# Half of each expert's down product in the full format, and three smaller moves

## The chip, the cores and the metric

One Trainium2 chip; the program runs on one of its cores. The metric is the device time of one execution, in microseconds (us). Before the change three runs gave 3543.78, 3550.85 and 3563.93 us, median 3550.85. Engines: PE (TensorE; PEld is its weight load), DVE (VectorE), ACT (ScalarE), POOL (GpSimd), SP (SyncE, which here issues the weight transfers).

## The reference, cut to what matters

One sequence of 256 tokens of width 1024 goes through a first block (a mixer, then a mixture of experts) and four layers of a second model, each of a gated feed-forward, a mixer and another gated feed-forward. Three parts matter here:

```
hdn = silu(einsum('td,edf->tef', xc, w1)) * einsum('td,edf->tef', xc, w3)   # experts, f = 256
y   = einsum('tef,efd->td', hdn * gate, w2)                                 # 128 tokens at a time
def rms_norm(x, g):     return x * rsqrt(mean(x * x, -1) + eps) * g
def swiglu(h, wi, wo):  a, b = split(h @ wi); return (silu(a) * b) @ wo     # 2816 hidden, 8 times
```

All weights are float32. Each token picks one of 4 groups of 8 experts and two experts in it.

## The kernel before, in words

**Split products.** A float32 matrix product is made of three matmuls in a reduced format, fp32r. The weights w are split into a high part (ACT copies w into a tile of type fp32r, which rounds) and a low part (DVE subtracts the high part from w); the activations are split in the same way. PE then adds high times high, high times low and low times high (`three`, L1857 in the experts, L1008 in the feed-forward). A matmul on plain float32 tiles, which needs no split, appears in the trace as two records of the same line.

**The expert stage** (`moe_stage`). 40 units: five windows of 128 token places, eight experts each. A unit's weights are 128 x 6144 floats (3 MB): four up pieces of 1024 columns (b = 0 to 3) and two down pieces (b = 4, 5), one for each half of the 256 hidden numbers. SP loads unit j + 2 into a ring of 4 slots when ACT has said that unit j - 2's slot is free (`act.nop()` at L2075, waited for in `load_ahead`, L443). Per unit j, in the written order of each engine:
- PE: up piece 0 (6 matmuls of 128 x 512), the transpose of the previous unit's hidden numbers (`turn_hidden`, L1872), up pieces 1 to 3, then `down_products(j - 1)`: two pieces, 6 matmuls each. After some units come `gather` (L1912), `turn_places` and `scatter_half` (L1926), in plain float32, for the next or the last window of tokens.
- ACT: high part of up piece 0, silu (L2000), high parts 1 to 3 (`high_part`, L1996), the nop that frees a slot, `hidden_high(j - 1)` (L2006), the high parts of the two down pieces of j - 1, then the issue of two transfers of 512 KB on its own queue (`load_quarters`, L2048).
- DVE: low part of up piece 0 (`low_part`, L2115), `product` (L2128), low parts 1 to 3, `hidden_low` (L2133), low part of down piece 4, one quarter sum, low part of down piece 5, one quarter sum. A quarter sum (L582) is a 128 x 1024 product of the adaptive-norm weights of layer 0 that has nothing to do with the experts; units 2 to 37 do two each, from the 512 KB transfers.
- The high parts sit in 4 tiles, used in turn by piece number: `up_piece` and `down_piece` give the number, 6 per unit, and ACT waits until piece number - 4 has been multiplied (`piece_used`).
- POOL adds each scattered half window to x (L2100).

**Root norm between stages** (`NextNorm` of kind "root", 12 places). ACT squares the eight chunks of x (L797), POOL adds them in pairs (`pair_sums`, L699, 128 x 256), PE sums each pair over features with a column of ones (`token_sums`, L711, 2 matmuls a pair), then DVE (L755), ACT, DVE (L758) and PE (`spread_tokens`, L720) make the inverse root and spread it; the next stage starts after that.

**The feed-forward stage** (`glu_stage`, 8 times, 11 units each). At its start PE clears four banks with matmuls on zeros (L1060, 4 of 128 x 512), then runs `first_up_products` (L1025): another zero matmul (L1027), pieces 0 and 1 chunk by chunk as DVE finishes each chunk of the normed input (`u_low`, L1231), then pieces 2 and 3. `up_products(1, 1)` and `down_products(0, 1)` follow; the latter is the first to add into the four cleared banks. Three of the eight stages (those before the mixers of layers 0 to 2) issue four transfers on ACT's queue during unit 1.

## Time and profile before

| | |
|---|---|
| median of three runs | 3550.85 us |
| the profiled execution | 3549.21 us, span 3547.4 us |
| PE busy | 3181.7 us, 90% |
| DVE busy | 2334.2 us, 66% |
| ACT busy | 1579.0 us, 45% |
| POOL busy | 145.4 us, 4% |
| mean granted TensorE clock | 0.924 of full |
| expert stage, units | about 280 to 726 us of the span |
| read from HBM | 690.27 MB, 196 GB/s over the span |

Time of PE is a union of overlapping matmuls: a record lasts from its start until its result is out, and the next one starts earlier. The pace of a row of matmuls is read from the difference of two starts, not from a duration. The same holds for ACT and DVE to a lesser degree.

### The profile page before, as it was taken

How to read it: one execution, taken by the hardware profiler on the slowest of the kernel's cores; microseconds unless marked ns; L12 is line 12 of the kernel's file. 1: busy time of each engine (PE TensorE's matmuls, PEld its weight loads, DVE VectorE, ACT ScalarE, POOL GpSimd, SP SyncE). 2: the span in 40 equal slices, each digit the busy share in tenths (PEclk: the TensorE clock that was granted, in tenths of full speed). 3: DMA queues.
4: the chain of work that ended last, by engine and by line, in shares of the span. 5: the costliest groups of instructions: out<-in, count | busy, mean ns of one | idle time of the engine just before them, and what ended most of it. 6: DMA issues, size and time to landing. Idle time of an engine off the chain costs nothing. (4 is left out here: it accounts for less than half of the span.)

```text
span 3547.4 us, 62682 instructions
## 1 busy us (share of the span) xinstructions
PE 3181.7 (90%) x26368; PEld 2947.7 (83%) x26368; DVE 2334.2 (66%) x3480; ACT 1579.0 (45%) x2254; POOL 145.4 (4%) x160
## 2 busy tenths in 40 slices
PE   7679888889897889999987799999899998978899
PEld 6577666679886789999985799999699998867899
DVE  6548899957765457677575467676667645655544
ACT  3426666644452244444552344444544444432443
POOL 0000000000101100000000000000000001011000
PEclk9869999989997989999995899999899999979899
DMA  9347999947620047677440167575157444200242
GB/s 388 128 160 277 355 381 381 366 190 304 241 97 37 2 157 305 238 279 306 156 163 1 72 230 308 227 303 214 39 201 307 187 178 174 109 37 3 107 178 83
DMA packets 74358, 697.79 MB, mean 197 GB/s; under 512 B 8080, under 2 KB 12176, under 8 KB 50704
## 3 DMA queue, kind: packets, MB, share of 16 engines
q1 hardware_dynamic: 31216, 532.99, 38.1%
q10 hardware_dynamic: 41760, 153.11, 11.5%
q0 software_dynamic: 1152, 8.39, 0.6%
q8 instruction: 173, 2.83, 0.3%
q14 instruction: 57, 0.47, 0.0%
HBM read 690.27 MB, written 4.19 MB: 196 GB/s over the span
## 5 line engine op out<-in xcount | busy, mean ns | idle before, releaser
L1171 DVE TENSOR_TENSOR w_split<-ring,w_split 128x1024 fp32r<-128x1024 f32 x513 | 625.7, 1223 | 446.5 <-ACT w_split L1082 444.1
L1082 ACT ACTIVATE w_split<-ring 128x1024 fp32r<-128x1024 f32 x513 | 540.2, 1056 | 769.8 <-PE banks L1012 605.8
L1010 PE MATMUL banks<-u_split,w_split 128*128 128x256 f32 x2816 | 802.5, 285 | 10.8 <-DVE u_split L1231 5.7
L1011 PE MATMUL banks<-u_split,w_split 128*128 128x256 f32 x2816 | 800.2, 284 | 0.0
L1012 PE MATMUL banks<-u_split,w_split 128*128 128x256 f32 x2816 | 800.0, 284 | 0.0
L1010 PEld LDWEIGHTS banks<-u_split,w_split 128*128 128x128 f32 x2816 | 544.8, 193 | 15.1 <-DVE w_split L1171 11.1
L1011 PEld LDWEIGHTS banks<-u_split,w_split 128*128 128x128 f32 x2816 | 544.4, 193 | 0.6
L1012 PEld LDWEIGHTS banks<-u_split,w_split 128*128 128x128 f32 x2816 | 544.0, 193 | 0.0
L582 DVE CUSTOM_DVE_ANT_0 bufs<-bufs 128x1024 f32<-128x1024 f32 x332 | 396.0, 1224 | 46.5 <-DMA bufs<-ada 32.6
L1010 PE MATMUL banks<-h_split,w_split 128*128 128x256 f32 x1408 | 398.7, 283 | 1.3 <-DVE w_split L1171 1.3
L1011 PE MATMUL banks<-h_split,w_split 128*128 128x256 f32 x1408 | 398.4, 283 | 0.0
L1012 PE MATMUL banks<-h_split,w_split 128*128 128x256 f32 x1408 | 398.4, 283 | 0.0
L518 PE MATMUL banks<-bufs_split,ring_split 128*128 128x256 f32 x1312 | 380.1, 290 | 0.0
L516 PE MATMUL banks<-bufs_split 128*128 128x256 f32 x984 | 292.8, 298 | 54.1 <-DVE ring_split L504 36.1
L2115 DVE TENSOR_TENSOR ring_split<-ring,bufs_split 128x1024 fp32r<-128x1024 f32 x240 | 296.0, 1260 | 19.1 <-ACT bufs_split L1996 18.9
L517 PE MATMUL banks<-bufs_split 128*128 128x256 f32 x936 | 274.6, 293 | 0.0
L1996 ACT ACTIVATE bufs_split<-ring 128x1024 fp32r<-128x1024 f32 x240 | 250.0, 1062 | 52.3 <-PE banks L1862 48.1
L1010 PEld LDWEIGHTS banks<-h_split,w_split 128*128 128x128 f32 x1408 | 270.3, 192 | 1.9 <-issue 1.9
L1012 PEld LDWEIGHTS banks<-h_split,w_split 128*128 128x128 f32 x1408 | 270.3, 192 | 0.0
L1011 PEld LDWEIGHTS banks<-h_split,w_split 128*128 128x128 f32 x1408 | 270.3, 192 | 0.0
L518 PEld LDWEIGHTS banks<-bufs_split,ring_split 128*128 128x128 f32 x1312 | 261.9, 200 | 0.0
L516 PEld LDWEIGHTS banks<-bufs_split 128*128 128x128 f32 x984 | 199.1, 202 | 64.4 <-DVE ring_split L504 39.3
(466 smaller groups left out, 5120.2 us busy)
## 6 DMA issues: line engine op xcount, KB each, us to landing
ring<-stream SPq DMA_DIRECT2D x155, 3072.0 KB, 11.0
bufs<-ada ACTq DMA_DIRECT2D x288, 512.0 KB, 10.4
bufs<-ada SPq DMA_DIRECT2D x7, 2048.0 KB, 11.7
bufs<-ada POOLq DMA_DIRECT2D x8, 1024.0 KB, 7.9
ring<-stream SPq DMA_DIRECT2D x2, 2688.0 KB, 9.8
bufs<-c_rows SPq DMA_DIRECT2D x8, 512.0 KB, 4.5
ring<-stream SPq DMA_DIRECT2D x1, 2704.0 KB, 12.5
ring<-stream SPq DMA_DIRECT2D x1, 2176.0 KB, 9.0
```

The lines of the kernel that those rows point to most:

```text
L516: pe.matmul(out, w_high, x_high, start=start, stop=False, skip_group_check=True)
L517: pe.matmul(out, w_high, x_low, start=False, stop=False, skip_group_check=True)
L518: return pe.matmul(out, w_low, x_high, start=False, stop=stop, skip_group_check=True)
L582: dve.tensor_tensor_reduce(w, w, c_row, 1.0, 0.0, ALU.mult, ALU.add, into).then_inc(done.sem, 1)
L1010: pe.matmul(out, w(0), x(0), start=start, stop=False, skip_group_check=True)
L1011: pe.matmul(out, w(0), x(1), start=False, stop=False, skip_group_check=True)
L1012: return pe.matmul(out, w(1), x(0), start=False, stop=stop, skip_group_check=True)
L1082: nc.scalar.activation(w_split[:, slot, 0, :], piece(j, b), ACT.Copy).then_inc(high.sem, 1)
L1171: e = nc.vector.tensor_tensor(w_split[:, slot, 1, :], piece(j, b), w_split[:, slot, 0, :].bitcast(F32), ALU.subtract)
L1996: act.activation(w_high[number % 4], piece(j, b), ACT.Copy).then_inc(high.sem, high.count(1))
L2115: dve.tensor_tensor(low_piece(j, b), piece(j, b), w_high[number % 4].bitcast(F32), ALU.subtract)\
```

## The change

Four edits. In the expert stage the second down piece (b = 5) is no longer split: PE multiplies it as plain float32, with the lower half of the turned hidden numbers copied by ACT to a plain float32 tile (`turned_f32`). Pieces are now numbered 5 per unit, `down_done` counts units whose down product is complete, and the nop that frees a ring slot stands behind `hidden_high(j - 1)`. In the root norm, POOL adds three pairs, and PE sums chunks 6 and 7 directly (`paired_sums`). In the feed-forward stage the four bank-clearing matmuls stand behind `first_up_products`.

```
-    for q in range(KC // 2):
+    for q in range(pairs):                      # NextNorm "root" passes pairs=KC // 2 - 1
...
+def paired_sums(core, pe, squares, bank, paired, squared, summed):
+    ones = core.const("ones")[:, 0:1]
+    for c in (0, 2, 4, 6, 7):
+        if c < KC - 2:
+            pe.wait_ge(paired.sem, paired.at(c // 2 + 1))
+        else:
+            pe.wait_ge(squared.sem, squared.at(c + 1))
+        for t in range(2):
+            last = pe.matmul(core.psum[:, bank + t, 0:1], squares[:, c, t * P:(t + 1) * P], ones, start=(c == 0), stop=(c == KC - 1))
+    last.then_inc(summed.sem, summed.count(1))
...
+            first_up_products()
             for b in range(4):
                 pe.matmul(core.psum[:, 4 + b, :], core.zeros[:, 0:P], core.zeros[:], start=True, stop=True)
-            first_up_products()
...
+    turned_f32 = [core.bufs[:, 8, (4 + 2 * q) * SEQ + P:(5 + 2 * q) * SEQ] for q in range(2)]
...
     def up_piece(j, b):
-        return 6 * j - 2 + b if j else b
+        return 5 * j - 1 + b if j else b
-    def down_piece(j, f):
-        return 6 * j + 8 + f if j < units - 1 else 6 * units - 2 + f
+    def down_piece(j):
+        return 5 * j + 8 if j < units - 1 else 5 * units - 1
...
+                number = down_piece(j)
+                pe.wait_ge(low.sem, low.at(number + 1))
+                for half in range(2):
+                    last = three(y[:, half, :], weight(number, j, 4, slice(half * 512, (half + 1) * 512)),
+                                 [h_split[:, j % 2, part, 0:P] for part in range(2)], e == 0, False)
+                last.then_inc(piece_used.sem, piece_used.count(1))
+                for half in range(2):
+                    last = pe.matmul(y[:, half, :], turned_f32[j % 2], piece(j, 5)[:, half * 512:(half + 1) * 512],
+                                     start=False, stop=e == E - 1, skip_group_check=True)
+                last.then_inc(down_done.sem, down_done.count(1))
...
-                    act.wait_ge(piece_used.sem, piece_used.at(down_ends(j - 2)))
-                act.activation(h_split[:, j % 2, 0, :], turned(j), ACT.Copy).then_inc(h_high.sem, h_high.count(1))
+                    act.wait_ge(down_done.sem, down_done.at(j - 1))
+                act.activation(turned_f32[j % 2], turned(j)[:, P:2 * P], ACT.Copy)
+                act.activation(h_split[:, j % 2, 0, 0:P], turned(j)[:, 0:P], ACT.Copy).then_inc(h_high.sem, h_high.count(1))
...
-                    if j >= 2:
-                        act.nop().then_inc(core.freed.sem, core.freed.count(1))
                 hidden_high(j - 1)
+                if 2 <= j < units:
+                    act.nop().then_inc(core.freed.sem, core.freed.count(1))
...
-                for f in range(2):
-                    high_part(j - 1, 4 + f, down_piece(j - 1, f))
+                high_part(j - 1, 4, down_piece(j - 1))
...
-                    if i == 1:
-                        low_part(j - 1, 5, down_piece(j - 1, 1))
```

DVE's `hidden_low` handles 128 instead of 256 columns.

ACT's order in one plain unit of the expert stage, before: the last line of the first unit's high parts, then the next unit (L1996 is a high part, L2000 the silu, L2006 `hidden_high`, L2048 the transfers).

```order
L1996 ACTIVATE bufs_split<-ring 128x1024
L2000 ACTIVATE bufs<-banks 128x256
L1996 ACTIVATE bufs_split<-ring 128x1024 x3
L2006 ACTIVATE bufs_split<-banks 128x256
L1996 ACTIVATE bufs_split<-ring 128x1024 x2
L2048 DMA bufs<-ada 128x1024 x2
```

ACT's order there after (L2009 is the high part, L2013 the silu, L2019 the plain copy of the lower half, L2020 the high part of the upper half, L2062 the transfers).

```order
L2009 ACTIVATE bufs_split<-ring 128x1024
L2013 ACTIVATE bufs<-banks 128x256
L2009 ACTIVATE bufs_split<-ring 128x1024 x3
L2019 ACTIVATE bufs<-banks 128x128
L2020 ACTIVATE bufs_split<-banks 128x128
L2009 ACTIVATE bufs_split<-ring 128x1024
L2062 DMA bufs<-ada 128x1024 x2
```

One high part of a weight piece is gone, and one small copy has come. The nop is not a row of this list: before, it stood behind the three high parts; after, it stands behind L2020.

PE's order after where a down product of the expert stage ends and the next unit begins (L1871 to L1873 are the split products, L1914 the plain ones).

```order
L1871 MATMUL banks<-bufs_split 128x512
L1872 MATMUL banks<-bufs_split 128x512
L1873 MATMUL banks<-ring_split_52,bufs_split 128x512
L1914 MATMUL banks<-ring,bufs 128x512 x2
L1871 MATMUL banks<-bufs_split 128x512
```

Before, six rows of L1860 to L1862 stood where L1914's two matmuls stand.

PE's order at the border between a mixer's last stage and a feed-forward stage, before (L711 and L720 are the norm's, L1060 and L1027 the zeros, L1010 to L1012 the products).

```order
L711 MATMUL banks<-consts_sb,bufs 128x1 x8
L720 MATMUL banks<-consts_sb,by_token 128x128 x2
L1702 UNCONDITIONAL_BRANCH
L1006 UNCONDITIONAL_BRANCH
L1060 MATMUL banks<-zeros_split 128x512 x4
L1027 MATMUL banks<-zeros_split 128x512
L1010 MATMUL banks<-u_split,w_split 128x256
```

And after (L725 for L711, L733 for L720, L1040 for L1027, L1023 to L1025 for the products).

```order
L725 MATMUL banks<-consts_sb,bufs 128x1 x10
L733 MATMUL banks<-consts_sb,by_token 128x128 x2
L1715 UNCONDITIONAL_BRANCH
L1019 UNCONDITIONAL_BRANCH
L1040 MATMUL banks<-zeros_split 128x512
L1023 MATMUL banks<-u_split,w_split 128x256
```

The norm has two matmuls more; the four zero matmuls have gone from here and stand 96 products later.

## Rows read from the trace of the kernel before

**Rows 1.** The page: mean busy share of the DMA engines in 40 slices, in tenths.

```profile
DMA  9347999947620047677440167575157444200242
```

**Rows 2.** Eight units: busy of PE, PEld, DVE, ACT, POOL; PEclk, DMA share, GB/s.

```profile
434.67:522.63 87.96, 78.45 (x354) 61.26 (x354) 82.99 (x100) 58.88 (x77) 4.80 (x2) 1.00 0.96 382
```

**Rows 3.** The DMA view of 434.67 to 522.63 us.

```profile
DMA packets 3462, 33.57 MB, mean 382 GB/s; under 512 B 383, under 2 KB 383, under 8 KB 2435
```

**Rows 4.** Timeline of DVE in the expert stage: start us, us, engine, line, operation.

```profile
434.67 0.47 DVE L2128 SCALAR_TENSOR_TENSOR bufs<-bufs,small,banks 128x256 f32<-128x256 f32 x1
435.06 3.49 DVE L2115 TENSOR_TENSOR ring_split<-ring,bufs_split 128x1024 fp32r<-128x1024 f32 x3
...
438.80 1.22 DVE L2115 TENSOR_TENSOR ring_split<-ring,bufs_split 128x1024 fp32r<-128x1024 f32 x1
439.93 1.22 DVE L582 CUSTOM_DVE_ANT_0 bufs<-bufs 128x1024 f32<-128x1024 f32 x1
...
444.50 0.47 DVE L2128 SCALAR_TENSOR_TENSOR bufs<-bufs,small,banks 128x256 f32<-128x256 f32 x1
```

**Rows 5.** Timeline of PE in the expert stage.

```profile
505.16 0.39 PE L1860 MATMUL banks<-bufs_split 128*128 128x512 f32 x1
505.38 0.39 PE L1861 MATMUL banks<-bufs_split 128*128 128x512 f32 x1
...
398.45 1.89 PE L1926 MATMUL banks<-bufs 128*128 128x256 f32 x8
```

**Rows 6.** Waits from 280 to 730 us: total, times, longest.

```profile
PE banks L1860 <- DVE ring_split L2115: 50.1, 55, 5.6
DVE bufs L582 <- DMA bufs<-ada: 7.8, 3, 4.8
```

**Rows 7.** Timeline of ACT, and landing of the ring's transfers (260 to 740 us).

```profile
411.41 1.06 ACT L1996 ACTIVATE bufs_split<-ring 128x1024 fp32r<-128x1024 f32 x1 [1.17 <-PE banks L1862]
413.97 0.39 ACT L2006 ACTIVATE bufs_split<-banks 128x256 fp32r<-128x256 f32 x1 [1.49 <-PE banks L1872]
416.76 1.06 ACT L1996 ACTIVATE bufs_split<-ring 128x1024 fp32r<-128x1024 f32 x1 [0.36 <-PE banks L1862]
...
421.23 1.06 ACT L1996 ACTIVATE bufs_split<-ring 128x1024 fp32r<-128x1024 f32 x1 [0.75 <-PE banks L1862]
...
DMA to landing us min/median/max: 9.9/11.8/13.6
```

**Rows 8.** Timeline of one root norm behind a feed-forward stage.

```profile
946.33 3.16 ACT L797 ACTIVATE bufs<-x_sb 128x256 f32<-128x256 f32 x8 [2.94 <-DVE x_sb L3700]
949.57 0.61 PE L711 MATMUL banks<-consts_sb,bufs 128*128 128x1 f32 x4 [0.18 <-POOL bufs L699]
951.23 0.61 PE L711 MATMUL banks<-consts_sb,bufs 128*128 128x1 f32 x4 [1.06 <-POOL bufs L699]
```

**Rows 9.** The same behind a mixer, and (745 us) behind the centering stage.

```profile
1287.84 0.81 ACT L797 ACTIVATE bufs<-x_sb 128x256 f32<-128x256 f32 x2 [0.93 <-DVE x_sb L2376]
1289.50 0.61 PE L711 MATMUL banks<-consts_sb,bufs 128*128 128x1 f32 x4 [0.60 <-POOL bufs L699]
...
745.00 2.02 PE L711 MATMUL banks<-consts_sb,bufs 128*128 128x1 f32 x8 [0.40 <-POOL bufs L699]
```

**Rows 10.** Feed-forward starts: zeros, first chunk, first product; a wait in unit 1.

```profile
1292.34 2.04 PE L1060 MATMUL banks<-zeros_split 128*128 128x512 f32 x4 [0.32 <-PEq L1702]
1293.46 0.48 DVE L1231 SCALAR_TENSOR_TENSOR u_split<-bufs,mod,u_split 128x256 fp32r<-128x256 f32 x1 [0.25 <-ACT u_split L824]
1294.61 0.41 PE L1010 MATMUL banks<-u_split,w_split 128*128 128x256 f32 x1
...
1513.36 0.39 PE L1010 MATMUL banks<-u_split,w_split 128*128 128x256 f32 x1 [2.24 <-DVE w_split L1171]
```

**Rows 11.** Two stretches of the first such start, columns as in rows 2.

```profile
1294.60:1297.20 2.60, 2.60 (x14) 2.59 (x13) 2.60 (x8) 1.76 (x4) 0.00 (x0) 0.50 1.11 403
1297.20:1300.00 2.80, 2.80 (x25) 2.80 (x25) 1.96 (x5) 1.07 (x3) 0.00 (x0) 0.99 1.00 418
```

More of the change, by code:

```diff
@@ L692, with pair_sums @@
 MEAN_BANK, ROOT_BANK = 2, 3
-def pair_sums(core, pool, squares, squared, paired, per=1, offset=0):
-    for q in range(KC // 2):
+def pair_sums(core, pool, squares, squared, paired, per=1, offset=0, pairs=KC // 2):
+    for q in range(pairs):
         pool.wait_ge(squared.sem, squared.at((2 * q + 2) // per + offset))
@@ L779, in on_gpsimd @@
         if self.kind == "root":
-            pair_sums(self.core, pool, self.squares, self.squared, self.paired)
+            pair_sums(self.core, pool, self.squares, self.squared, self.paired, pairs=KC // 2 - 1)
     def on_tensor(self, pe):
@@ L790, in on_tensor @@
             inverse = core.event("inverse")
-            token_sums(core, pe, self.squares[:, 0:KC:2, :], self.bank, self.paired, self.summed, n=KC // 2)
+            paired_sums(core, pe, self.squares, self.bank, self.paired, self.squared, self.summed)
             pe.wait_ge(inverse.sem, inverse.at(self.turn + 1))
@@ L1809, in up_piece @@
     def up_piece(j, b):
-        return 6 * j - 2 + b if j else b
-    def down_piece(j, f):
-        return 6 * j + 8 + f if j < units - 1 else 6 * units - 2 + f
+        return 5 * j - 1 + b if j else b
+    def down_piece(j):
+        return 5 * j + 8 if j < units - 1 else 5 * units - 1
     def up_ends(j):
         return up_piece(j, 3) + 1
-    def down_ends(j):
-        return down_piece(j, 1) + 1
     def piece(j, b):
@@ L1838, in moe_stage @@
             "u_high", "u_low", "w_high", "w_low", "piece_used", "glu_silu", "glu_hidden", "norm_applied", "h_high", "h_low"))
-        y_done = core.event("glu_down_done")
+        y_done, down_done = core.event("glu_down_done"), core.event("expert_down_done")
         step, ada_loaded = core.event("ada_step"), [core.event(f"ada_loaded{q}") for q in range(4)]
@@ L1895, in down_products @@
                     pe.wait_ge(y_copied.sem, y_copied.at(2 * w))
-                for f in range(2):
-                    number = down_piece(j, f)
-                    pe.wait_ge(low.sem, low.at(number + 1))
-                    for half in range(2):
-                        last = three(y[:, half, :], weight(number, j, 4 + f, slice(half * 512, (half + 1) * 512)),
-                                     [h_split[:, j % 2, part, f * P:(f + 1) * P] for part in range(2)],
-                                     e == 0 and f == 0, e == E - 1 and f == 1)
-                    last.then_inc(piece_used.sem, piece_used.count(1))
+                number = down_piece(j)
[8 more added lines that the diff above has]
+                last.then_inc(down_done.sem, down_done.count(1))
             def gather(w):
@@ L2022, in copy_y @@
             def copy_y(w):
-                act.wait_ge(piece_used.sem, piece_used.at(down_ends(E * w + E - 1)))
+                act.wait_ge(down_done.sem, down_done.at(E * w + E))
                 if w:
@@ L2084, in _ @@
                     scale_y(v - 1, e - 2)
-                for f in range(2):
-                    high_part(j - 1, 4 + f, down_piece(j - 1, f))
+                high_part(j - 1, 4, down_piece(j - 1))
                 if e == 5 and v < WINDOWS - 1:
@@ L2132, in hidden_low @@
                 dve.wait_ge(h_high.sem, h_high.at(j + 1))
-                dve.tensor_tensor(h_split[:, j % 2, 1, :], turned(j), h_split[:, j % 2, 0, :].bitcast(F32), ALU.subtract)\
+                dve.tensor_tensor(h_split[:, j % 2, 1, 0:P], turned(j)[:, 0:P], h_split[:, j % 2, 0, 0:P].bitcast(F32), ALU.subtract)\
                     .then_inc(h_low.sem, h_low.count(1))
@@ L2204, in _ @@
                 hidden_low(j - 1)
-                low_part(j - 1, 4, down_piece(j - 1, 0))
-                for i, q in enumerate(ada_quarters(j)):
+                low_part(j - 1, 4, down_piece(j - 1))
+                for q in ada_quarters(j):
                     if q == 0:
                         dve.wait_ge(c_ready.sem, c_ready.at(1))
-                    if i == 1:
-                        low_part(j - 1, 5, down_piece(j - 1, 1))
                     sum_quarter(q)
-                if not ada_quarters(j):
-                    low_part(j - 1, 5, down_piece(j - 1, 1))
             step.made += quarters
```

## The prediction

> **What bounds the kernel now.** The page comes first. PE is busy 90% of the span and ends the chain of waits, so in the feed-forward stages and mixers only PE's own work counts. But one stretch is unlike the rest: slices 4 to 8 (some 280 to 730 us) have the DMA engines at nine tenths or more in four of five [rows 1]. That is the expert stage, on which the large edit acts. I read it in stretches: eight units (434.67 to 522.63, one window of tokens) take 87.96 us, with DVE busy 82.99 us, PE 78.45 us and ACT 58.88 us, the clock at full and the DMA share 0.96 at 382 GB/s [rows 2]. Two things are nearly full there at once, DVE and DMA. The timeline tells which of them sets the pace: from one `product` to the next in a plain unit DVE has no gap, 434.67 to 444.50, 9.83 us [rows 4]: six low parts at a pitch of 439.93 - 438.80 = 1.13 us, two quarter sums at about the same, two short operations. The waits agree: PE waited 50.1 us in all for low parts, while DVE waited only 7.8 us for a transfer [rows 6]. So DVE sets the pace of plain units, five of the eight. The other three take (87.96 - 5 x 9.83) / 3 = 12.9 us each: in two DVE also waits for ACT and shares with POOL while a scattered half is added, in one PE does `gather`.
>
> **Expert stage, DVE and ACT.** One low part per unit goes (1.13 us), and `hidden_low` is halved, which I take at 0.13 us from its 0.33 us pitch: 9.83 - 1.26 = 8.57 us for DVE. ACT loses a high part of 1.06 us [rows 7] and gains a copy; it has 29 us of idle in 88 [rows 2], so that is worth nothing by itself.
>
> **Expert stage, PE.** Split matmuls of 512 columns start 0.22 to 0.23 us apart (505.16, 505.38 [rows 5]); I use 0.228. Six of them go, 1.37 us. Two plain matmuls of 512 columns come, which the trace doesn't show in this width. The nearest row is 256 columns wide: eight records, four matmuls, in 1.89 us of which the last record's own length is about 0.38, so (1.89 - 0.38) / 7 = 0.216 us a record, 0.43 us a matmul [rows 5]; twice the columns, 0.86 us each, 1.73 us for two. The bounds are 0.43 us each (as if width cost nothing) and 1.2 us each. I take 0.86, since the split rows at 256 and 512 columns also scale by width. PE gains 1.73 - 1.37 = +0.36 us a unit. Before: 36 x 0.228 and some 0.2 for the transpose, 8.4 us; after 8.8, and with a small gap where formats change 8.95 us. So PE would set the plain unit at 8.95 us, 0.88 below now. The two scatter units lose the low part's 1.13 each, the gather unit, which PE bounds, perhaps 0.2. A window: 5 x 0.88 + 2 x 1.13 + 0.2 = 6.9 us less, 81.1 us.
>
> **What is late next: the transfers.** A window moves 33.57 MB [rows 3]. At 382 GB/s with a share of 0.96 [rows 2] the engines would give 398 GB/s if never idle: 33.57 MB / 398 GB/s = 84.3 us. That is above 81.1, so the transfers take over. The other end is the best stretch at full share in my rows, 418 GB/s [rows 11]: 80.3 us, and then PE's 81.1 counts. I take 84.3, since it has the same mix of large and small packets: 3.7 us a window. Some 37 of the 40 units have this rhythm, 4.67 windows: 17 us. The last two units have no quarter sums, PE bounds them, +0.4 us each. The stage: **-16 us**, bounds -32 (81.1 everywhere) and 0.
>
> The later nop works against it. It stood at the dispatch of the third high part, now it stands behind `hidden_high`, which waits for PE's transpose: 411.41 against 413.97, 2.6 us later in a plain unit [rows 7]. Before, a slot was freed 421.23 - 416.76 = 4.5 us into ACT's unit, two units after the slot's first use, so a load had 2T - 4.5 us to land, 15.2 us at T = 9.83 against a median of 11.8 and at most 13.6 [rows 7]. After, it has 2T - 7.1, which at T = 10.5 (a window of 84.3) is 13.9 us. The cover shrinks from 3.4 to 2.1 us over the median; I cost that at nothing because the load behind is then queued already, so the engines don't fall idle. If the cover is gone, see the fourth rival.
>
> **Root norm.** Behind a feed-forward stage (7 places) the squares are done at 946.33 + 3.16 = 949.49, PE's third pair starts at 949.57, but the fourth pair comes from POOL only at 951.23, because DVE runs a long subtraction beside it [rows 8]. After: four records of the third pair at a pitch of 0.13 us, then eight more, 949.57 + 12 x 0.13 + 0.09 = 951.2 against 951.84: 0.6 us. In four of the seven the last pair ran at half clock (as the pairs of rows 9 with 2.02 / 2 = 1.01 us, not 0.61) since PE had idled; there up to 1.0. I take 0.75, 5.2 us. Behind a mixer (4 places) the last squares are ready at 1288.65, PE starts at 1289.50; chunk 6 can go first, the end moves from 1290.11 to 1289.4: 0.7 us, 2.8 us in all [rows 9]. Behind the centering stage PE is itself the slow one, at half clock, 2.02 us for two pairs [rows 9]: one more chunk costs +0.9 us. Sum **-7 us**, bounds -9 and -4. DVE, ACT, DVE and PE follow one after the other, so it all counts.
>
> **The zero matmuls.** Before, four of them took 2.04 us at half clock where PE had nothing else until the first chunk, ready at 1293.46 + 0.48 = 1293.94; the first product began at 1294.61 [rows 10]. After, they stand where PE is full: 4 x 0.216 = 0.87 us at full clock. Three stages absorb that, because PE waits in unit 1 for a low part held up behind ACT's transfers (2.24 us at 1513.36 [rows 10]). In three others the first product can start 0.67 us sooner, three matmuls, worth 0.36 us at the later pace. 5 x 0.87 - 3 x 0.36 = +3.3 us. The clock adds to it: products ran at 0.50 until 1297.2 and at 0.99 from there [rows 11], after PE had been fed with zeros from 1292.34. Now PE stands idle for two more microseconds before. "TensorE: Matmul & The Clock Gate" of the Trainium skill (section on what's actually happening) says that the throttled state is the default and activity releases it, so idling could put the rise off. I add 0.7 us: **+4 us**, bounds 0 and +12.
>
> **The sum.** -16 - 7 + 4 = -19 us. The profiled execution took 3549.2 us, 1.6 below the median of the three runs: 3550.85 - 19 = 3532 us.
>
> **Rivals.** What a measurement can tell from no change is about 0.5%, 17.8 us: faster is below 3533, slower above 3569.
>
> First, the transfers keep up (they ran at 418 GB/s in one full stretch, rows 11; ring loads and the small packets would overlap more if a load were always waiting). Then PE bounds the window at 81.1 us: -32 - 7 + 4 = -35, 3516 us. Against it: the share is 0.96 already.
>
> Second, the transfers are the true bound already and DVE's fullness only keeps step: the stage gives some 3 us, -3 - 7 + 4 = -6, 3545 us. For it: 0.96 of share, and a later nop. Against it: DVE has no gap in the plain unit [rows 4], and waits 7.8 us in all [rows 6]. "DMA: Bandwidth & Descriptors" of the Trainium skill (section "Where 436 GB/s comes from") states some 358 GB/s as the limit from HBM to one core. By it the window's 33.57 MB would need 93.8 us; it takes 87.96, so this trace is past that figure, and only the direction of this rival is left of it.
>
> Third, the moved zeros cost more: each of five starts keeps half clock for a microsecond or two longer, +12 instead of +4, and the norm gives 5: -16 - 5 + 12 = -9, 3542 us.
>
> Fourth, on the other side, the ring starves. A load must land within 2T - 7.1 us (less in a gather unit, where the transpose comes later still). As the queue fills, landing grows; from 2 x 11.0 - 7.1 = 14.9 us on, the present mean unit of 11.0 can't be held. At 16 us of landing T = 11.5, +1.7 on each of five plain units, less 2.5 in the others: +6 a window, +27, and with the rest +24: 3575 us. Against it: landing was at most 13.6 us, and grows mostly when a load waits behind another, which is no idleness. For it: both halves of the cover are measured, and it is thin.
>
> **Chances.** Forecast 0.44, first rival 0.16, second 0.22, third 0.07, fourth 0.11. The forecast lies just past the border, so 0.27 of its 0.44 is faster and 0.17 is same; the first rival is faster; the second 0.02 faster and 0.20 same; the third same; the fourth slower. Faster 0.45, same 0.44, slower 0.11. The low end of the range takes in most of the first rival, 3511; the high end the second and third, 3551. The forecast's own range is 3523 to 3541.
>
> **What would show it.** In the profile after: eight units of the expert stage in about 84 us with the DMA share near 1.00; fewer DVE and PE waits on low parts, and waits of ACT on ring transfers or DVE on the 512 KB transfers in their place; L1914's records 0.43 us apart; DVE's plain unit with gaps. The last sum of a norm 0.6 to 1.0 us earlier; four zero matmuls at 0.216 us pitch inside the feed-forward start, and the clock's rise there no later than now. I am wrong if the window stays at 88 us with gaps on DVE (second), falls to 81 (first), or grows with ACT waiting for the ring (fourth).

## The result, and the profile after

The changed kernel took 3569.17 us (median of six runs), the kernel before 3549.56 us beside it: ratio 1.0058, 95% interval 1.0032 to 1.0084. That is some 20 us slower, where 19 us less were forecast. The profiled execution's span is 3569.9 us, before 3547.4 us, so this pair of traces holds the loss, 22.5 us.

Where it went was read first. The start of DVE's norm sums, set against the same sums of before, moves by -2.1 us ahead of the expert stage and by +33.1 us behind it; from there to the end some 11 us come back in small steps, the largest 4.5 us. So one stage loses 35 us. In it, three windows of eight units of the changed kernel (columns as in [rows 2], which show one window of before with a DMA share of 0.96):

```profile
369.87:660.47 290.60, 245.81 (x1015) 183.11 (x1014) 221.03 (x271) 150.44 (x232) 14.37 (x6) 0.94 0.87 346
```

The same 24 units of before:

```profile
374.65:640.80 266.15, 237.37 (x1062) 185.21 (x1062) 249.12 (x295) 176.99 (x231) 14.41 (x6) 0.99 0.94 371
```

DVE has 28 us less work, as meant, and the stage is 24 us longer. No engine is full any more, and neither are the transfers: their share fell from 0.94 to 0.87. Something waits, and the list of waits (engine, tile and line; released by; total us, times, longest; 280 to 745 us) says what:

```profile
PE banks L1871 <- DVE ring_split L2128: 67.7, 21, 9.4
DVE bufs L582 <- DMA bufs<-ada: 62.8, 19, 7.4
ACT bufs_split L2009 <- DMA ring<-stream: 30.2, 14, 4.1
```

Against [rows 6], DVE's wait for the 512 KB transfers rose from 7.8 to 62.8 us, and a wait of ACT for ring loads has come. PE's wait is the second one's shadow: a low part stands behind the quarter sum on DVE. The units themselves are of two kinds. A unit with nothing late, from product to product, takes 8.56 us:

```profile
501.05 0.47 DVE L2141 SCALAR_TENSOR_TENSOR bufs<-bufs,small,banks 128x256 f32<-128x256 f32 x1
509.61 0.46 DVE L2141 SCALAR_TENSOR_TENSOR bufs<-bufs,small,banks 128x256 f32<-128x256 f32 x1
```

Against [rows 4] that is 1.27 us less, just DVE's saving. But of 39 units, seven take 15.7 to 18.6 us. This is how one begins (timeline: start, us, engine, line, operation, in brackets the idle time before and its releaser; SPq and ACTq are issues of transfers):

```profile
515.55 0.33 SPq L450 DMA_DIRECT2D ring<-stream  x1
515.68 0.27 ACT L2020 ACTIVATE bufs_split<-banks 128x128 fp32r<-128x128 f32 x1
515.74 0.33 ACTq L2062 DMA_DIRECT2D bufs<-ada  x1
...
526.70 1.21 DVE L2128 TENSOR_TENSOR ring_split<-ring,bufs_split 128x1024 fp32r<-128x1024 f32 x1
531.37 1.22 DVE L582 CUSTOM_DVE_ANT_0 bufs<-bufs 128x1024 f32<-128x1024 f32 x1 [3.46 <-DMA bufs<-ada]
```

and what follows on DVE, PE and ACT:

```profile
539.05 1.23 DVE L582 CUSTOM_DVE_ANT_0 bufs<-bufs 128x1024 f32<-128x1024 f32 x1 [6.45 <-DMA bufs<-ada]
541.57 0.77 PE L1871 MATMUL banks<-bufs_split 128*128 128x512 f32 x1 [9.40 <-DVE ring_split L2128]
544.89 0.28 ACT L2019 ACTIVATE bufs<-banks 128x128 f32<-128x128 f32 x1 [10.43 <-PE banks L1883]
544.93 0.33 SPq L450 DMA_DIRECT2D ring<-stream  x1
545.09 0.33 ACTq L2062 DMA_DIRECT2D bufs<-ada  x1
```

The ring load (3 MB) and the first of the two 512 KB transfers are issued 0.2 us apart. DVE is ready for the quarter at 531.37 - 3.46 = 527.91, 12.2 us after the issue; it lands 15.6 us after it. The next pair is later still: DVE waits 6.45 us, PE 9.40 us for DVE's low part, ACT 10.43 us for PE's transpose, and only then comes the free, and with it the next ring load, again beside the next 512 KB transfers. All 34 pairs of issues from 300 to 740 us stand within 0.3 us of a ring load's issue. Before, the pair stood 3.8 us or more away from it in every case, and its lead in a plain unit was much the same, 449.76 - 438.15 = 11.6 us (the issue, and the first sum that uses it):

```profile
438.15 0.82 ACTq L2048 DMA_DIRECT2D bufs<-ada  x2
...
449.76 1.22 DVE L582 CUSTOM_DVE_ANT_0 bufs<-bufs 128x1024 f32<-128x1024 f32 x1
```

What the two queues do to each other shows in the DMA view of 517 to 524 us, behind that issue (queue: packets, MB, share of 16 engines; q1 is SP's ring, q10 ACT's):

```profile
q1 hardware_dynamic: 91, 2.24, 78.7%
q10 hardware_dynamic: 85, 0.34, 13.0%
```

About one packet each, 91 to 85, but a packet of the ring is 24.6 KB and one of the other queue 4.0 KB. So the second queue gets 0.34 MB in 7 us, 49 GB/s, and its 1.05 MB can't be through before the ring's 3.15 MB are: 3.15 MB at 2.24 / 7 = 320 GB/s take 9.8 us, in which 0.48 MB of the other pass; the rest comes behind. Before, the small packets passed where the ring load was nearly through. It had been issued at 433.28 us, the pair at 438.15; from 438 to 441 us the ring's packets move alone (first line), from 442 to 444 us the pair's do, beside the last of the ring's:

```profile
q1 hardware_dynamic: 49, 1.20, 93.5%
...
q10 hardware_dynamic: 114, 0.47, 76.1%
q1 hardware_dynamic: 19, 0.07, 9.0%
```

Landings from 300 to 740 us say the same (min/median/max; 512 KB transfers, then ring loads):

```profile
DMA to landing us min/median/max: 11.5/13.5/22.9
DMA to landing us min/median/max: 10.1/13.0/14.7
```

Before, the 512 KB transfers landed in 4.9/8.7/18.3 us, the ring's as in [rows 7]. The lead, from a transfer's issue until DVE is ready for it, was 13.8 us at the median before and is 14.8 now, so it is the landing that changed: 3 of the transfers came late before, 19 now. The Trainium skill, "DMA: Bandwidth & Descriptors" (section "Queues, rings and completion order"), says that each DMA engine goes round between its queues packet by packet. As an estimate from that rule and the two packet sizes, the queue of small packets beside one of packets six times as large would get a seventh of the bytes; the trace agrees (85 of 176 packets, 0.34 of 2.58 MB).

The norm's edit did what was worked out. Behind a feed-forward stage (compare [rows 8]):

```profile
980.39 3.16 ACT L810 ACTIVATE bufs<-x_sb 128x256 f32<-128x256 f32 x8 [2.95 <-DVE x_sb L3709]
983.63 1.50 PE L725 MATMUL banks<-consts_sb,bufs 128*128 128x1 f32 x12 [0.17 <-POOL bufs L699]
```

From the start of the squares to the end of the last sum it takes 983.63 + 1.50 - 980.39 = 4.74 us, before 951.84 - 946.33 = 5.51.

The moved zeros cost more clock than was worked out. At the start that [rows 11] show, products ran at half clock for 3.3 us, before for 2.6 (first line below, granted clock 0.50). But at a start right behind another feed-forward stage the clock was at full almost from the first product before (second line, the kernel before), and now stays at half for five microseconds (third line, the same start now):

```profile
1322.90:1326.20 3.30, 3.27 (x15) 3.30 (x16) 3.30 (x9) 2.04 (x4) 0.00 (x0) 0.50 1.06 366
...
1495.30:1500.60 5.30, 4.35 (x35) 4.08 (x35) 4.95 (x11) 3.06 (x7) 0.00 (x0) 1.00 1.05 411
...
1522.30:1527.60 5.30, 5.30 (x25) 5.30 (x26) 4.96 (x12) 3.10 (x6) 0.00 (x0) 0.50 1.03 378
```

Before, four zero matmuls more had run on PE just ahead. Summed over the eight starts, products ran at half clock for 17.1 us before and for 33.7 us now. It is the zeros that do it: with the norm's edit alone it was 19.6 us, with the zeros moved as well 33.3 us. The price is small: the first 96 products of a stage took 102.8 us before and 106.9 now, summed over the eight, and 3.8 us come back because the first product starts sooner. With the zeros' own time, the 250th product stands 2.7 us later behind the norm, in all.

### The profile page after: what moved, and what is told of

Its sections match the earlier page's. It is cut to its first block and busy times, and to the rows that moved or that the text cites. A ratio compares the mean times of both kernels' runs of the same rounds, so it can differ in the third digit from the quotient of the medians.

```text
span 3569.9 us, 62566 instructions
## 1 busy us (share of the span) xinstructions
PE 3192.6 (89%) x26336; PEld 2943.8 (82%) x26336; DVE 2287.7 (64%) x3440; ACT 1535.5 (43%) x2254; POOL 130.6 (4%) x148
## 3 DMA queue, kind: packets, MB, share of 16 engines
q1 hardware_dynamic: 31216, 532.99, 38.1%
## 5 line engine op out<-in xcount | busy, mean ns | idle before, releaser
L1023 PE MATMUL banks<-u_split,w_split 128*128 128x256 f32 x2816 | 805.5, 286 | 14.5 <-DVE u_split L1244 12.9
L1025 PE MATMUL banks<-u_split,w_split 128*128 128x256 f32 x2816 | 803.2, 285 | 0.0
L1023 PEld LDWEIGHTS banks<-u_split,w_split 128*128 128x128 f32 x2816 | 547.9, 195 | 19.4 <-DVE w_split L1184 9.8
L1025 PEld LDWEIGHTS banks<-u_split,w_split 128*128 128x128 f32 x2816 | 547.4, 194 | 0.0
L1023 PE MATMUL banks<-h_split,w_split 128*128 128x256 f32 x1408 | 398.7, 283 | 1.3 <-DVE w_split L1184 1.3
L1025 PE MATMUL banks<-h_split,w_split 128*128 128x256 f32 x1408 | 398.4, 283 | 0.0
L516 PE MATMUL banks<-bufs_split 128*128 128x256 f32 x984 | 291.7, 296 | 49.6 <-DVE ring_split L504 31.8
L517 PE MATMUL banks<-bufs_split 128*128 128x256 f32 x936 | 273.8, 293 | 0.0
L1023 PEld LDWEIGHTS banks<-h_split,w_split 128*128 128x128 f32 x1408 | 270.3, 192 | 1.9 <-issue 1.9
L1025 PEld LDWEIGHTS banks<-h_split,w_split 128*128 128x128 f32 x1408 | 270.3, 192 | 0.0
L2128 DVE TENSOR_TENSOR ring_split<-ring,bufs_split 128x1024 fp32r<-128x1024 f32 x200 | 247.7, 1270 | 33.6 <-ACT bufs_split L2009 33.3
L1871 PE MATMUL banks<-bufs_split 128*128 128x512 f32 x400 | 173.7, 434 | 71.0 <-DVE ring_split L2128 70.5
## 6 DMA issues: line engine op xcount, KB each, us to landing
ring<-stream SPq DMA_DIRECT2D x155, 3072.0 KB, 11.2
```

The costliest lines, as they stand in the source:

```text
L516: pe.matmul(out, w_high, x_high, start=start, stop=False, skip_group_check=True)
L517: pe.matmul(out, w_high, x_low, start=False, stop=False, skip_group_check=True)
L1023: pe.matmul(out, w(0), x(0), start=start, stop=False, skip_group_check=True)
L1025: return pe.matmul(out, w(1), x(0), start=False, stop=stop, skip_group_check=True)
L1871: pe.matmul(out, x_high, w_high_, start=start, stop=False, skip_group_check=True)
L2128: dve.tensor_tensor(low_piece(j, b), piece(j, b), w_high[number % 4].bitcast(F32), ALU.subtract)\
```

## Experiments

Theory T: the late free puts the ring load and the 512 KB transfers on the engines together, the second queue loses, and DVE's quarter sums come too late. Rivals: R1, the late free starves the ring itself; R2, the faster order asks for more than the transfers can give wherever the free stands; R3, PE's plain products cost too much.

**The small edits alone, and the expert stage alone.** The first is the changed kernel with the `moe_stage` of before. The second is the changed kernel with the norm and the zero matmuls of before.

> The changed kernel with the expert stage of the kernel before: only the root norm's last pair and the moved zero matmuls are left of the change. In the trace of the changed kernel the expert stage took 34 to 35 us more, while everything behind it gave some 11 us back. All theories on the expert stage expect the same here: the stage as before, 425 to 427 us from its first product to its last, and the whole 5 to 12 us below the kernel before (ratio 0.9965 to 0.9985). If the 4 us that the centre of the mixer stages gave back were an echo of the longer expert stage (the clock, or loads further ahead), they are missing here and the ratio is nearer 0.999.

Measured: 0.9973 (0.9959 to 0.9988), stage 425.2 us from first product to last, before 425.8.

> The changed kernel with the root norm and the zero matmuls as before: only the expert stage is changed. Every theory on the stage expects it as slow as in the changed kernel, about 460 us from first product to last, and the whole 26 to 36 us above the kernel before (ratio 1.0075 to 1.010). If it were under 1.005, the small edits would hold part of the loss.

Measured: 1.0058 (1.0039 to 1.0077). The loss is in the expert stage, but the size missed what I expected, and so did the stage, 436.5 us in this execution and not 460. The stage's length differs by 23 us between these two executions, with how often the chain above is set off (here 14 waits of DVE, 38.1 us in all); the landing of the 512 KB transfers, 13.3 us at the median, is as in the changed kernel. From here on I read landings and waits, and leave the total to the ratios. Multiplied, the parts give 0.9973 x 1.0058 = 1.0031 against 1.0058 for the whole. That is just below its interval, but the parts have intervals of their own, so no gap between the parts and the whole is shown.

**The norm alone** (zeros and experts as before).

> The kernel before with the root norm's edit alone (expert stage and zero matmuls as before). With the zero matmuls moved as well it was 0.27% below the kernel before. If the norm gives 7 us and the zeros cost 4, as forecast, this is 0.9960 to 0.9975, below the pair of both; if the zeros gave something too, it is 0.9980 to 0.9995.

Measured: 0.9984 (0.9969 to 0.9998). That is not where I expected it with a norm that gives 7 us and zeros that cost 4, but where I had put zeros that give something too; the two intervals overlap, so by time alone the zeros can't be told from nothing. Within the stages the traces tell them. From the norm's reciprocal on DVE to a stage's 250th product, summed over the eight starts, it takes 339.6 to 340.1 us in five traces with the zeros where they were (a sixth, the expert stage alone, has 342.7) and 342.3 to 344.4 us in nine with the zeros moved: a cost of some 3 us. From norm to norm, the eight stretches with a feed-forward stage are 5.5 us shorter here than before. But the expert stage alone, with neither edit, is 3.4 us longer in the same stretches, so one trace doesn't carry such a sum to the microsecond.

**The free moved, each way.** In the changed kernel, back behind the third high part:

```
                         high_part(j, b, up_piece(j, b))
+                    if j >= 2:
+                        act.wait_ge(down_done.sem, down_done.at(j - 1))
+                        act.nop().then_inc(core.freed.sem, core.freed.count(1))
                 hidden_high(j - 1)
-                if 2 <= j < units:
-                    act.nop().then_inc(core.freed.sem, core.freed.count(1))
```

> The changed kernel with one line back: ACT frees the ring slot behind the third high part again, ahead of hidden_high (with a wait for the down products that read the slot in place, which are nearly always done by then). Theory T (the late free issues the ring load together with the two 512 KB transfers of the second queue; these share the engines, land later than DVE's quarter sums need them, and DVE, PE and the next free follow): the 512 KB transfers land in 9 to 10 us at the median instead of 13.5, DVE's wait on them falls from 63 us to under 20, the stage falls from 460 us to 400 to 426, the whole to 3505 to 3545 us. Rival R1 (the late free starves the ring load itself): nearly the same gain, but the landing of the 512 KB transfers stays at 13 us and only ACT's wait on the ring (30 us) goes. Rival R2 (the faster order of work asks for transfers sooner than the engines can give, wherever the free stands; the two quarter sums stand back to back now): the stage stays above 445 us and DVE goes on waiting over 40 us. Rival R3 (the plain products cost PE more than worked out): the stage stays at 460 us, PE full.

Measured: 1.0001 (0.9987 to 1.0015), 3548.39 us, landing 4.0/10.1/21.4 us, stage 426.8 us, each just past the edge of T's range. In the kernel before, the same nop moved behind `hidden_high` and nothing else:

> The kernel before with one line moved: ACT frees the ring slot behind hidden_high, as the changed kernel does, all arithmetic as before. T: the landing of the 512 KB transfers rises from 8.7 us at the median to 12 or more, DVE begins to wait on them (over 30 us, before 8), and the whole is 15 to 40 us longer (ratio 1.004 to 1.011). R1: longer as well, by ACT's wait on the ring. R2 and R3: no change (ratio within 0.999 to 1.002), since the order of work and the products are the old ones.

Measured: 1.0057 (1.0038 to 1.0076), landing 9.9/11.7/21.2 us: the ratio as T expected, landing and DVE's wait a little less. The waits of the two (the early free first, then the kernel before with the late one):

```profile
DVE bufs L582 <- DMA bufs<-ada: 31.8, 8, 6.9
ACT bufs_split L2009 <- DMA ring<-stream: 2.6, 4, 0.8
```

```profile
DVE bufs L582 <- DMA bufs<-ada: 23.2, 9, 6.2
ACT bufs_split L1996 <- DMA ring<-stream: 5.8, 5, 1.7
```

The late free alone, in the old arithmetic, costs 0.57%; taken out of the changed kernel it gives 0.57%. That one moved line is the whole loss. R3 is out: PE was busy for 245.81 of 290.60 us in the changed kernel. But the early free did not reach what T said: DVE still waits 31.8 us, and against the small edits alone (0.9973) the new arithmetic still costs 0.3%. Its leads are no shorter than those of before (14.5 us at the median, 13.8 before), its landings are longer (10.1 us, 8.7 before). Two things differ: the transfers are asked for every 8.56 us in a row of plain units instead of every 9.83, which is R2, and the pair's issue stands 1.9 us behind the ring's instead of 3.9, since ACT has one high part less between them. No run parts the two.

**No second queue.** The 512 KB transfers but the first four are left out, and DVE sums what lies there.

```
                 for q in ada_quarters(step_of):
...
+                    if q < 4:
                         act.dma_start(ada_slot[:, (q % 4) * D:(q % 4 + 1) * D], ...)
...
+                if q < 4:
                     dve.wait_ge(ada_loaded[q % 4].sem, ...)
```

> The changed kernel without the 512 KB transfers of the second queue after the first four (68 of 72 are left out; DVE sums what lies in the slots, without waiting for them). What is left is the rhythm of the engines with the ring loads alone, 3.15 MB a unit. T and R2 (the second queue is the one that comes late): no unit longer than 13.2 us, five of eight at 8.6 to 9.0, a window 82 to 86 us, the stage 395 to 405 us instead of 460, the whole 3500 to 3515 us. R1 (the late free starves the ring load itself): ACT goes on waiting for the ring, over 20 us, and units of 15 us and more stay. R3 (PE's plain products are the price): the stage stays above 440 us with PE full and no unit under 9.5 us.

Measured: 3503.6 us, ratio 0.9867 (0.9840 to 0.9894), stage 391.0 us, 4 us under what I expected. 24 units:

```profile
371.65:617.75 246.10, 235.76 (x1015) 176.81 (x1014) 219.35 (x272) 150.91 (x232) 14.42 (x6) 1.00 0.79 307
```

All three windows took 82.0 us, unit for unit the same (four of eight units at 8.6 to 8.8 us, not five, and one at 9.7), and ACT waited 0.8 us for the ring. R1 is out: with the late free the ring keeps up when it is alone. (This run also has 36 MB less to fetch, so its gain is no offer.)

**The 512 KB transfers ahead of the late free.** In the changed kernel, the issue alone is moved:

```
                         high_part(j, b, up_piece(j, b))
+                if j + 1 > first_quarter + 1:
+                    load_quarters(j + 1)
                 hidden_high(j - 1)
...
-                if j + 1 > first_quarter + 1:
-                    load_quarters(j + 1)
```

> The changed kernel, its late free kept, with the issue of the two 512 KB transfers for the next unit moved ahead of hidden_high, so they stand in their queue before the ring load does. T (the second queue comes late because it shares with the ring load issued beside it): DVE's wait on them falls from 63 us to under 35 us and the whole is 10 to 25 us below the changed kernel (ratio to before 0.9985 to 1.003). R1: ACT's wait on the ring (30 us) stays or grows and the whole doesn't fall (ratio 1.005 to 1.009).

Measured: 3524.19 us, 0.9948 (0.9928 to 0.9969), better than T's range, landing 5.2/9.5/22.2 us, stage 405.6 us. 24 units and the waits:

```profile
365.96:623.52 257.56, 239.76 (x1014) 178.91 (x1014) 219.85 (x271) 150.09 (x231) 14.42 (x6) 0.99 0.97 391
...
ACT bufs_split L2009 <- DMA ring<-stream: 37.0, 17, 3.3
PE banks L1871 <- DVE ring_split L2128: 26.9, 18, 4.1
DVE bufs L582 <- DMA bufs<-ada: 14.8, 4, 5.6
```

ACT's wait for the ring is longer than in the changed kernel and the whole is 1.1% shorter: the wait for the ring was not the loss, the one for the second queue was. The four transfers that are still late here are alike: each is the second of its pair, lands after 18.5 to 22.2 us, and has the next ring load issued 12 us behind it, in a row of plain units. The same in the kernel before with the late free:

> The kernel before with the late free, which alone cost 0.57%, and the 512 KB transfers issued ahead of it. T (the late free hurts because the ring load and the second queue's transfers are issued together, and the second queue loses): most of the loss goes, ratio 0.998 to 1.002, DVE's wait on the second queue under 10 us. R1 (the late free is too late for the ring itself): the loss stays, 1.004 or more, with ACT waiting for the ring.

Measured: 0.9993 (0.9972 to 1.0013), landing 4.2/6.9/15.2 us, and DVE doesn't wait for these transfers once. The late free costs nothing if the small queue has a head start. So R2 is not what the changed kernel lost by: at 391 GB/s the transfers can give more than they gave it (346). But with a share of 0.97 they are what bounds the kernel with the right order; there R2 holds.

**Is it the edit or the order of issues?** The kernel before with its early free, the 512 KB transfers directly ahead of it:

> The kernel before with the two 512 KB transfers issued behind the third high part, directly ahead of the free (which stays where it was). There DVE sets the pace of plain units at 9.8 us and waits only 8 us for these transfers, so T expects next to nothing: ratio 0.997 to 1.001. Set against the changed kernel with the same order of issues (0.9948), it tells what the edit of the arithmetic is worth where the transfers stand right: some 0.3 to 0.6%. If the gain of that run came from the order of issues alone and the edit gave nothing, this run is at 0.995 too.

Measured: 1.0005 (0.9986 to 1.0024). The order alone gives the old arithmetic nothing, though landing rose to 13.0 us: at 9.8 us a unit and with the issue a few us sooner (lead 18.5 us at the median) there is time for it (one wait, 3.2 us). So 0.9948 is not the order's gain alone.

**Both early, in three ways.** The issue behind silu with the early free; then the pair with both behind the third high part, 512 KB first or the ring's free first.

> Both issues early: the ring slot is freed behind the third high part, as in the run with the early free, and the two 512 KB transfers of the next unit are issued right behind silu, some 8 us sooner than now. With the early free alone five or six units of a stage still took 14 to 18 us, each with DVE waiting for a 512 KB transfer (32 us in all). If that is lateness of a queue that is squeezed while a ring load runs, the longer lead takes it away: DVE's wait under 10 us, the stage 400 to 412 us, the whole 3520 to 3535 us, which is below both kernels (ratio 0.993 to 0.997). If the engines' sum of transfers is the bound (R2: some 380 GB/s, 4.19 MB a unit, 11.0 us a unit whatever the order), the stage stays at 420 to 428 us and the waits go over to the ring (ratio 0.999 to 1.001).

> The changed kernel with both issues behind the third high part, the 512 KB transfers first, the ring's free directly behind them. Its pair has the two swapped and nothing else. If the order of the two in the engines decides: 0.992 to 0.996, landing of the 512 KB transfers 9.5 us or less at the median, DVE's wait on them under 16 us.

> The changed kernel with both issues behind the third high part, the ring's free first, the 512 KB transfers directly behind it. If the order of the two in the engines decides: landing of the 512 KB transfers 12 us or more at the median, DVE's wait on them over 25 us, ratio 0.998 to 1.003. If only the lead counts (how long before its use a transfer is issued), it is as good as its pair, 0.992 to 0.996.

Measured: 0.9935 (0.9911 to 0.9959); 0.9956 (0.9938 to 0.9974); 0.9984 (0.9963 to 1.0006). The ratios fell where expected. For the first two the waits did not: DVE still waited 24.2 and 27.6 us, at landings of 10.8 and 12.1 us, and the stage of the first took 417.2 us. The third waited 32.7 us at a landing of 13.1, as expected if the order decides. The swap in the last pair is worth something: the runs were taken side by side, ten each, with medians of 3531.95 and 3541.66 us and means 10 us apart (3 to 17). It moves landing by 1.0 us and the lead by 1.7. It is not order by itself, though: with the 512 KB transfers first, the free's issue comes 1.8 us behind theirs.

**More head start**, after this: the late free, the issue behind silu.

> The changed kernel, its late free kept, with the issue of the two 512 KB transfers behind silu: three high parts (some 3.2 us) ahead of where the run with the ratio 0.9948 had it, so some 6 us ahead of the ring load instead of 3. If what counts is how long these transfers run before a ring load joins them (landing at the median was 6.9 to 9.5 us with a head start, 12 to 13 us without one, whichever was issued first): landing 8 us or less at the median, DVE's wait on them under 10 us, the stage 398 to 408 us, ratio 0.990 to 0.995. If the order alone counts and the two transfers gain nothing from more lead: landing and ratio as in that run, 9 to 10 us and 0.994 to 0.996. If ACT's wait for the slots (its issues wait for DVE's sums) eats the lead, as it did in part in the run with both issues early: landing falls and the ratio is 0.996 or more.

Measured: 3513.49 us, 0.9929 (0.9901 to 0.9958), stage 401.4 us, landing 5.0/10.0/21.6 us:

```profile
367.27:622.62 255.35, 239.18 (x1014) 177.53 (x1014) 220.92 (x272) 151.57 (x233) 14.39 (x6) 0.99 0.97 395
...
DVE bufs L582 <- DMA bufs<-ada: 11.2, 5, 3.4
```

Landing did not fall to the 8 us that I expected; the issue now comes in the middle between two ring issues. The wait is 3.6 us less than with the issue ahead of `hidden_high`, in one trace each, which shows no difference. All runs of the stage together (gap: median from the nearest ring issue to the first of the two 512 KB issues, minus is ahead of it; landing and lead at the median; DVE's wait for them; the 24 units):

| kernel | free | gap | landing | lead | DVE waits | 24 units | ratio |
|---|---|---|---|---|---|---|---|
| before | early | +3.9 | 8.7 | 13.8 | 7.8 | 266.2 | 1 |
| its 512 KB first | early | -1.3 | 13.0 | 18.5 | 3.2 | 266.5 | 1.0005 |
| its free late | late | +1.4 | 11.7 | 14.3 | 23.2 | 288.8 | 1.0057 |
| late, 512 KB first | late | -2.8 | 6.9 | 18.5 | 0 | 263.9 | 0.9993 |
| changed kernel | late | +0.1 | 13.5 | 14.8 | 62.8 | 290.6 | 1.0058 |
| free early | early | +1.9 | 10.1 | 14.5 | 31.8 | 274.3 | 1.0001 |
| ring, then 512 KB | early | 0.0 | 13.1 | 17.5 | 32.7 | 273.8 | 0.9984 |
| 512 KB, then ring | early | -1.8 | 12.1 | 19.2 | 27.6 | 273.6 | 0.9956 |
| 512 KB at silu | early | -2.9 | 10.8 | 19.8 | 24.2 | 265.0 | 0.9935 |
| 512 KB first | late | -3.6 | 9.5 | 19.1 | 14.8 | 257.6 | 0.9948 |
| 512 KB at silu | late | +4.1 or -4.4 | 10.0 | 19.9 | 11.2 | 255.4 | 0.9929 |

What counts is each transfer's lead less its landing. Where that is below nothing DVE waits, and over the 68 transfers the shortfalls come to DVE's whole wait (7.8 of 7.8 us before, 62.4 of 62.8 in the changed kernel); a landing of 13.0 us costs 3.2 us at a lead of 18.5, and one of 13.5 costs 62.8 at 14.8. The medians alone don't rank the runs, since it is the latest few that cost.

The last four beat both kernels; between them the intervals mostly don't decide. What the expert stage's arithmetic is worth is told by two pairs with the same order of issues: 0.9993 and 0.9948 (late free, 512 KB first), 1.0005 and 0.9956 (both early, 512 KB first). That is 0.45 and 0.49% for all the edits, of which the small ones alone have 0.27. Some 0.2% is left for the arithmetic, 7 us, less than the 0.3 to 0.6% that I expected, with intervals about as wide.

## Why the prediction was wrong

**What failed is one sentence**, on the later nop: "I cost that at nothing because the load behind is then queued already, so the engines don't fall idle." I weighed the nop against the ring's own cover only. Its price was elsewhere: it moved the ring load's issue onto the issue of the 512 KB transfers, which got 49 GB/s beside it, and their landing rose from 8.7 to 13.5 us, against a lead of 12.2 us in the unit shown. Forecast at nothing, the moved line measured 0.57% of the whole, 20 us. The lines that would have told it were all there: DVE's 7.8 us of waits for these transfers [rows 6], a landing of 8.7 us against 11.6 of lead in a plain unit, and 2435 of 3462 packets under 8 KB [rows 3]. I had asked how long a ring load takes, not what it does to what flies beside it. And the engines did fall idle, share 0.87, because a late quarter holds DVE, PE, ACT and so the next free.

**The fourth rival named the right line and the right sign** (3575 us), with the wrong victim. It said that the ring starves. ACT's waits for the ring did come (30.2 us), but with the small queue first they are longer (37.0 us) in a kernel 1.1% faster. That its 3575 us lies near the measured 3569 is luck.

**The expert stage's other terms held in part.** DVE's plain unit: 8.57 us worked out, 8.56 measured. PE was to set it at 8.95: it doesn't, the plain unit runs at DVE's pace. The plain matmul: 0.86 us worked out, and its two records do come 0.43 us apart; with the change of format behind them two matmuls took 458.53 - 456.71 = 1.82 us.

```profile
456.71 1.88 PE L1914 MATMUL banks<-ring,bufs 128*128 128x512 f32 x4
458.53 0.47 PE L1871 MATMUL banks<-bufs_split 128*128 128x512 f32 x1
```

A window of work without a late transfer: 81.1 us worked out, 82.0 measured without the second queue. In part that is luck. Against the window of [rows 2], the five plain units gave 5.2 us and not 4.4, and the two scatter units, forecast at 1.13 us each, gave 0.4 each. A window with the transfers as the bound: 84.3 worked out at 398 GB/s; with the 512 KB transfers first it is 257.56 / 3 = 85.9 us at 391 GB/s and a share of 0.97.

The stage's -16 us was a forecast of that kernel, which the changed kernel never became. Even there it holds only in part: its stage, 405.6 us, is 11 us shorter than that of the kernel before with the same free and order (708.99 - 291.94 = 417.1), and in the total some 7 us are left for it beside the small edits. That 0.9948 is 18 us, where 19 were forecast, is a sum of a stage that gave less and small edits that gave more.

**The small terms.** Norm -7: of it 5.2 us stood for the seven norms behind a feed-forward stage, whose stretches are 5.4 us shorter with the norm's edit alone, and +0.9 for the one behind the centering stage, measured +0.7; the four behind mixers can't be read in stretches that vary by far more. Zeros +4: some 3 us in the traces. But its terms were off: the clock was to cost 0.7 us through one longer start, and the half clock lasted 16.6 us longer over eight, at 4.2 us for the first products; the third rival's "a microsecond or two longer" at a start was right about the clock, and the earlier first products paid for most of it. The sum, -3, lies a little outside what was measured for the two edits together, 0.27% or 10 us (4 to 15). In that run's trace 5.2 us of it lie in one stretch, the third mixer's (148.2 us before); the expert stage alone, with neither edit, has 3.0 us less there as well, so the cause stays open.

**The 4.5 us that the first mixer gave back show no effect.** That stretch (1290.6 us less 952.3 in the trace of before) took 330.6 to 345.8 us in fifteen profiled executions, in which hardly an instruction of it differs; among them 335.2 to 345.8 us in the five with all of it as before. Without the experiments it would have passed for a result.

## What to carry to other kernels

A moved signal moves a transfer's start: list every transfer in flight at the new time, on all queues, and for each one its lead (from issue to first use) less its landing. Where a queue with small packets runs beside one with large packets, issue the small one some microseconds ahead, or well behind, but not together. And taking work off an engine moves together what it issues: with the early free kept, one high part less on ACT brought the pair from 3.9 to 1.9 us behind the ring's issue, and the median landing went from 8.7 to 10.1 us. A cover of 2.9 us in a plain unit (11.6 - 8.7) was gone with that and one moved free.

## What was not expected of the hardware

- Two queues with work shared the engines by packets, 91 to 85 in 7 us, and so by bytes 2.24 to 0.34 MB.
- No packet of a pair issued at 438.15 us moved before 441 us. So an issue 4.9 us behind a ring load's put it where that load was nearly through.
- A transfer issued beside a 3 MB load landed with it or behind it: 13.5 against 13.0 us at the median, for a sixth of its size.
- One late transfer nearly doubled a unit (15.7 to 18.6 us, where the run without the second queue has 8.6 to 9.7), since the signal that starts the next load stands at the end of the same chain.
- The transfers can give 395 GB/s over 255 us with both queues at work, at a share of 0.97.
- With four zero matmuls fewer ahead of them, the first products of three stages ran at half clock for 5.0 to 5.5 us, where it had been 0.2 to 0.7.
